# Two-block transformer kernel: where the q and k sums of squares are asked for in the attention stretch

## The reference

```
h = modulate(rms(x)); u = h @ w_in           # fq, fk, fv, fg, dq, dk, dv
q = q * rsqrt(mean(q*q over 64) + EPS) * g   # per head of 64, the same for k
fox:  softmax(q k^T / 8 + c_t - c_s) v       # 8 heads, c = cumsum(log_sigmoid(fg + b))
diff: (softmax(q1 k1^T/8 + alibi) - lam * softmax(q2 k2^T/8 + alibi)) v   # 4 heads
x = x + g1 * (concat(fox, rms(diff)) @ w_out)
```

## Time and profile before

| | |
|---|---|
| median of 3 runs | 973.07 us (968.74 to 983.04) |
| profiled execution | 978.75 us, span 976.9 us |
| granted TensorE clock, mean | 0.974 |
| busy, share of the span | PE 94%, PE weight loads 91%, DVE 68%, ACT 54%, POOL 24% |
| DMA | 203.03 MB, mean 208 GB/s |

### The profile page before, as it was taken

The page is one execution under the profiler, slowest core; times in us unless marked ns, Lnnn a source line. Parts: engine busy times, 40 slices in busy tenths (PEclk is TensorE's granted clock), DMA queues, the critical chain, the costliest instruction groups (busy, mean ns, idle before and its releaser), DMA issues. The chain is left out here.

```text
span 976.9 us, 17993 instructions
## 1 busy us (share of the span) xinstructions
PE 919.1 (94%) x7508; PEld 889.1 (91%) x7508; DVE 663.4 (68%) x874; ACT 526.2 (54%) x801; POOL 232.4 (24%) x231
## 2 busy tenths in 40 slices
PE   3889999999999999889999999997889799999998
PEld 3889999999999999889999999886778799999998
DVE  5889995664466687666688667678986758544442
ACT  4377656457856544345665343446786454444331
POOL 3200003333334221236565011300003333111100
PEclk9779999999999999999999999979999889999999
DMA  9645554443576688864778887354535638455460
GB/s 361 283 158 172 190 175 171 137 157 127 205 240 216 216 285 293 282 218 148 250 276 306 289 299 267 129 177 148 190 137 191 232 120 317 173 184 194 162 216 22
DMA packets 37008, 203.03 MB, mean 208 GB/s; under 512 B 5952, under 2 KB 6976, under 8 KB 18112
## 3 DMA queue, kind: packets, MB, share of 16 engines
q1 hardware_dynamic: 36928, 201.89, 58.5%
HBM read 200.82 MB, written 1.05 MB: 207 GB/s over the span
## 5 line engine op out<-in xcount | busy, mean ns | idle before, releaser
L1199 DVE TENSOR_TENSOR w_lo<-raw,w_hi 128x2048 fp32r<-128x2048 f32 (+1 forms) x144 | 326.7, 2269 | 185.4 <-ACT w_hi L625 185.4
L979 PE MATMUL acc<-uh,w_hi 128*128 128x256 f32 x1392 | 397.8, 286 | 8.3 <-DVE w_lo L1199 6.5
L979 PE MATMUL acc<-ul,w_hi 128*128 128x256 f32 x1392 | 390.5, 281 | 0.0
L979 PE MATMUL acc<-uh,w_lo 128*128 128x256 f32 x1392 | 390.3, 280 | 0.0
L625 ACT ACTIVATE w_hi<-raw 128x2048 fp32r<-128x2048 f32 (+1 forms) x144 | 270.2, 1876 | 86.8 <-PE acc L979 86.2
L979 PEld LDWEIGHTS acc<-uh,w_hi 128*128 128x128 f32 x1392 | 264.5, 190 | 14.2 <-DVE w_lo L1199 6.9
L979 PEld LDWEIGHTS acc<-uh,w_lo 128*128 128x128 f32 x1392 | 265.8, 191 | 0.0
L979 PEld LDWEIGHTS acc<-ul,w_hi 128*128 128x128 f32 x1392 | 264.4, 190 | 0.3 <-issue 0.2
L979 PE MATMUL acc<-hidh,w_hi 128*128 128x256 f32 x432 | 120.1, 278 | 0.0
L979 PE MATMUL acc<-hidl,w_hi 128*128 128x256 f32 x432 | 120.1, 278 | 0.0
L979 PE MATMUL acc<-hidh,w_lo 128*128 128x256 f32 x432 | 120.1, 278 | 0.0
(11 more groups left out here) (310 smaller groups left out, 1460.9 us busy)
## 6 DMA issues: line engine op xcount, KB each, us to landing
raw<-in_tiles SPq DMA_DIRECT2D x138, 1024.0 KB, 4.9
colw<-in_ada_cols SPq DMA_DIRECT2D x80, 512.0 KB, 5.3
ada_w<-in_ada_tiles SPq DMA_DIRECT2D x8, 1024.0 KB, 12.8
raw<-in_rest SPq DMA_DIRECT2D x4, 768.0 KB, 5.1
cact<-in_c_rows SPq DMA_DIRECT2D x2, 512.0 KB, 5.3
xT<-in_x SPq DMA_DIRECT2D x1, 1024.0 KB, 9.2
out<-xT SPq DMA_DIRECT2D x8, 128.0 KB, 3.1
par_all<-in_params SPq DMA_DIRECT2D x1, 372.0 KB, 5.2
```

The costliest lines, as they stand in the source:

```text
L979: ins = pe.matmul(o, l, r, start=(s.k == 0 and i == 0 and not j), stop=(s.last and i == s.kts - 1 and j == 2))
L1199: dve.tensor_tensor(lo, raw_of(n), hi.bitcast(F32), ALU.subtract).then_inc(S("lo_ready"), 1)
```

## The change

The sum of squares of a q or k step is asked for in the second half of the following step (nb 1) instead of the first, on TensorE and with it ScalarE's root. VectorE's scaling moves from nb 1 of the following step to nb 0 of the step after that. The first two pairs of scores move from half steps 6 and 8 to 7 and 9, and the transposes of heads 0 and 1 from 9 and 11 to 10 and 12. The number and kind of instructions stays the same, and so does the wait of L831.

```
-    S_AT = {6: 0, 8: 1, 12: 2, 14: 3, 16: 4, 18: 5, 20: 6, 22: 7}
-    T_AT = {9: 0, 11: 1, 15: 2, 17: 3, 19: 4, 20: 5, 21: 6, 22: 7, 23: 8, 24: 9, 25: 10, 26: 11}
+    S_AT = {7: 0, 9: 1, 12: 2, 14: 3, 16: 4, 18: 5, 20: 6, 22: 7}
+    T_AT = {10: 0, 12: 1, 15: 2, 17: 3, 19: 4, 20: 5, 21: 6, 22: 7, 23: 8, 24: 9, 25: 10, 26: 11}
...
     # ScalarE
-                    if nb == 0 and prev in ("dq", "dk", "fq", "fk"):
+                    if nb == 1 and prev in ("dq", "dk", "fq", "fk"):
                         jq += 1
                         act.wait_ge(S("qsum_done"), jq)
...
     # TensorE
-                    if nb == 0 and n and steps[n - 1].kind in ("dq", "dk", "fq", "fk"):
+                    if nb == 1 and n and steps[n - 1].kind in ("dq", "dk", "fq", "fk"):
                         take("M0")
                         pe.wait_ge(S("qsq"), NB * (jq + 1))
...
     # VectorE
-                    prev = steps[n - 1] if n else None
-                    if nb == 1 and prev and prev.kind in ("dq", "dk", "fq", "fk"):
+                    prev = steps[n - 2] if n > 1 else None
+                    if nb == 0 and prev and prev.kind in ("dq", "dk", "fq", "fk"):
                         jq += 1
                         dve.wait_ge(S("qroot"), jq)
```

## The result

The changed kernel took 1009.6 us (998.5 to 1013.9, 4 runs) against 978.06 us (968.7 to 983.9, 4 runs): ratio on record 1.030, interval 1.021 to 1.038. It is slower, by 29 us as the ratio has it and by 31.5 us between the two medians; the forecast was 27 us and 1000 us.

The account below looks back on a forecast made before the run. VectorE was taken to bound the attention stretch from 664 to 726.2 us. Before pair 2 1.0, the two rounds 9.6 and 11.6, and the clock 4.8 made 27 us, so 1000 us from 973.07; range 986 to 1010.

Parts of the forecast that it names:

- The time: Whole kernel: 27 us slower, 1000 us from a median of 973.07.
- the entry: Stretch before pair 2's maps: they start 1.0 us later, although the cumulated gates are done about 3.6 us earlier.
- the clock: TensorE at half rate behind pauses ahead of scores of pairs 2, 4 and 6: 4.8 us, bounds 0 and 9.
- What bounds the kernel: VectorE from 664 to 726.2 us, busy 60.60 of 62.20; TensorE's closing chain passes any delay on one for one.
- The Square waits for a sum that moved: ScalarE's Square of a step's first half waits for the previous step's later sum: 8 to 10 us before fk0's.
- The ring's size: Attention pairs 2 to 6: Square's wait and later scaling make engines wait in turn, 9.6 plus 11.6 us at full clock.
- the rounds: From maps of pair 2 to those of pair 4, then to those of pair 6: 9.6 and 11.6 us longer.
- the signs named: VectorE waits about 5 us before reciprocals of pairs 2 and 4; its busy share from 664 to 726 near 0.7.
- Rival C: Attention stretch: VectorE's work stays the pace at 9.65 us a step, only an early gain remains: 969.5 us; chance 0.10.
- Rival A: Attention stretch: the same engine waits, but TensorE's clock stays at full rate: 22.2 us, so 995; chance 0.20.
- rival B: Attention stretch: the same engine waits with TensorE's clock at half for most of it: 34 us, so 1007; chance 0.13.

Follow-up runs that it names:

- experiment 9: Kernel before, with the column sums of the 13 attention steps over 64 of 1024 columns, so its result is not the reference's: ratio 0.990.
- warm: Changed kernel plus matmuls whose result nobody reads, in TensorE's pauses ahead of the scores of pairs 0, 2, 4 and 6: ratio 1.023 against the kernel before.
- experiment 8: Changed kernel plus matmuls whose result nobody reads, ahead of TensorE's wait for the scaling; the same run as warm: ratio 1.023 against the kernel before.
- experiment 5: Changed kernel with VectorE's scaling put back into the second half of the following step; sum, root and scores stay late: ratio 1.033 against the kernel before.
- experiment 3: Kernel before with only VectorE's scaling moved half a step later; sum, root and scores stay: ratio 1.033.
- experiment 6: Changed kernel with alternate halves of sq and VectorE's scaling back, leaving the later sum, root and first scores: ratio 1.025 against the kernel before.
- scale_only: Kernel before with only VectorE's scaling moved half a step later; the same run as experiment 3: ratio 1.033.
- two_sq_scale_back: Changed kernel with alternate halves of sq and VectorE's scaling back; the same run as experiment 6: ratio 1.025 against the kernel before.
- scores_back: Changed kernel with the first two pairs of scores and their transposes where they were: ratio 1.028 against the kernel before.
- short_cols: Kernel before with attention steps' column sums over 64 of 1024 columns; the same run as experiment 9: ratio 0.990.
- cols_early: Kernel before with the later first two pairs of scores and the column sums of seven attention steps made earlier, all complete: 968.64 us, ratio 0.993.

## Why the prediction was right, step by step

- **The time.** The stretch grew by 31.7 us for 27. By the medians 1009.6 is 9.6 above the 1000 forecast and only 0.4 below the end of the range, 1010; that it came inside is luck. About half of the 9.6 is the kernel before, whose median was 978.06 in these runs and 973.07 in those that I went by. The other half is the entry and the clock, below.
- **What bounds the kernel, right.** The closing chain passed the delay on (175.27 us in both), and VectorE set the pace of the stretch (experiment 9).
- **The Square waits for a sum that moved, right.** 12.26 and 11.39 us in the changed kernel; freeing it gave back 12.1 of 31.7 us. The forecast of "8 to 10 us" for that wait was short, because TensorE's products behind the pause ran at half clock: in warm the same two waits are 9.87 and 9.17 us.
- **The ring's size, right.** With the clock mostly back (experiment 8) the rounds lost 20.8 us for 9.6 + 11.6 = 21.2 walked, and all of it 22.4 for 22.2. The walk counts pair 4's scores as 1.40 us in the first round and as 1.0 in the second; that moves 0.3 to 0.4 us between the rounds and leaves their sum. Of the signs named, the wait ahead of pair 2's reciprocals came (5.43 us), pair 4's was smaller (3.91 for about 5), and VectorE fell to 0.67 for 0.7.
- **The entry, wrong in size.** +1.0 walked, +4.9 measured. The gates' sums were taken over at 664.70 - 3.25 = 661.45, 2.9 us earlier than in the earlier trace rows for 3.6 walked (in warm it is 3.6), so that gain came. What I missed is the pause of 2.40 us ahead of pair 0's scores, after which the clock was low again (0.50 from 660 to 664). Experiment 8 gave back 3.3 us of the entry: 2.6 ahead of pair 2's scores, which is this miss, and 0.7 in those scores, which the prediction has in its clock term. The remaining 0.7 us stays open.
- **The clock, undersized.** 4.8 us forecast, with 9 as upper bound; 9.2 measured. Pair 2's scores and the rounds make 6.7 of it for the 4.8; the rest is that entry. The Trainium skill ("TensorE: Matmul & The Clock Gate", Part 1) has the array fall to its lower clock when it is idle. The windows of experiment 8 against the changed kernel's, 1.00 against 0.64, agree.
- **Rival C fell**, and with it the reading that the busiest engine's instructions decide. VectorE had 97% of the window from 664 to 726.2 us and the same instructions afterwards, and the stretch took a quarter longer. Rival A (full clock, 22.2) was the size of the ring, but not of the run. The clock came nearer to rival B's 9 us than to my 4.8.
- **What I had not seen at all:** the move of sum and root alone (with the Square's wait that it brings), or of the scaling alone, costs as much as the whole change (experiments 5 and 3), and the later root without the Square's wait still costs 24 us (experiment 6). The prediction says of the Square's wait and the later scaling that "together they close a ring". The moves are not summands but alternatives: as I read the traces, each of them puts exponentials, `split_hi` and `split_lo` in series with the scaling. The old order had kept it between maps and reciprocals, where it covered the exponentials.

## What to carry to other kernels

Ahead of moving an instruction group to a later place in the queues, list every wait that counts on its old place, buffer reuse above all: a wait that the edit does not touch (here line 831) can come to mean something else. Where an engine is busy for 97% of a stretch, what matters of its order is which of its instructions cover the others' answers; the same work in another order cost 24 to 32 us here, and the parts of such a loss overlap, so that undoing one of them may give nothing back. Price the clock along with any pause that a change opens.

## What the runs showed of the hardware

The matmul pitch, the time from one start to the next, took two values at a granted clock of 1.00. The closing chains of 1488 matmuls took 175.27 us, 117.8 ns each, in six executions, those before and after among them; in the other six (scale_only, two_sq_scale_back, scores_back, warm, short_cols, cols_early) the same chain took 168.65, 113.3 ns each. Last chains of the kernel warm:

```profile
822.76 168.65 PE acc L981 x1488
```

Within one execution it can differ between stretches: from 590 to 604 us the starts were 113.4 ns apart in the profile before and 117.8 ns in the one after, in w_down steps that are the same in both. The changed kernel's column sums show the lag grow there: it came 0.46 us early to the one at 498.72 (499.18 before) and 4.53 us late to the one at 622.24 (617.71 before), mostly by some 0.2 us more at each. Of this lag 3.25 us were left at dq0. Such stretches may also be much of the spread of 15 us between runs of one kernel; what sets the pitch was not tested.

The length of a pause alone did not tell the clock behind it. It stayed at 1.00 behind 3.22 us and was low behind 2.40 us in the changed kernel. Behind a pause of 1.85 us ahead of a sum the clock stayed at 1.00 in the changed kernel (680 to 684) and was at 0.60 around the same sum in warm (676 to 680).
